# Norm, turning and router logits of a mixture-of-experts layer in one pipeline, and the router in one block

## The chip, the cores and the metric

The kernel runs on one core of a Trainium2 chip. The metric is the device time of one execution in microseconds (us), as the median of several runs. Engines: TensorE (PE, with its weight loads as PEld), VectorE (DVE), ScalarE (ACT), GpSimd (POOL), and SyncE (SP), which issues most of the DMAs.

## The reference, cut to what matters

Two transformer blocks over 1024 tokens of 1024 channels, float32. The change touches the head of the first block's mixture of experts (64 experts in 8 groups, top 2, hidden width 256):

```
h = rms_norm(x, norm_ffn)                       # 1024 x 1024
g_logits = h @ w_group + b_group                # 8 columns
g_sel, g_weight = argmax and its softmax share
e_logits = (h @ w_expert + b_expert)[group g_sel]   # 64 columns, 8 kept
top_w, top_local = top 2 of e_logits, softmax * g_weight
y = sum over both experts of weight * (silu(t @ w_gate) * (t @ w_up)) @ w_down
```

The assignments are sorted into blocks of 128 rows by expert; every expert's weights (3 MB) are read once.

## The kernel before, in words

The program is a sequence of blocks. In a block every engine runs its own list of instructions and waits on semaphores; at its end all engines meet. `c.recycle(0)` adds a block in which GpSimd clears and frees semaphores. `do = c.chain(...)` makes an engine wait for its own last instruction.

`moe_first` works through these stages for x, which lies in SBUF as 8 tiles (m) of 128 rows:

1. `load` fetches the norm's gain and waits for it. A further block issues the four loads of the router's weights `wr` (72 columns: 8 groups, 64 experts) and `bias` on SP.
2. `norm_transpose` (line 176): ScalarE squares and sums all 8 tiles, takes one root over all, and VectorE inverts it; then ScalarE scales tile m into one of 2 buffers `normed` and permutes its channels on the way (line 205: it writes single values 128 apart), SP stores the scaled tile to `ffn_rows` in DRAM (line 237), TensorE turns it in 8 pieces (line 228), VectorE multiplies it by the gain into `hT` (line 216). Reuse of a buffer waits for the turning and the store.
3. `route` (line 1787): SP issues the weights of the first two pairs of experts (12 DMAs of 1 MB), while TensorE makes the logits: for each m and k, hT is the stationary operand (128 columns), wr the moving one (72) (line 1813). The next blocks choose the group and both experts on VectorE, rank every assignment within its expert by matmuls with ones and a triangle (lines 1893, 1896), place them (lines 1907 to 1943), and turn the placement into lists `slot_tok`, `slot_row` with 16 one-hot matmuls (line 1950). There are seven blocks, so seven meetings. The third pair's weights are issued in the second.
4. The expert loop: `ExpertSteps` with 3 weight slots of a pair of experts and 32 steps. `clear_rows` zeroes the 3 row buffers in a block of its own (line 2346). GpSimd gathers 128 rows of `ffn_rows` per step and scatters results; TensorE turns the rows (line 2064) and makes the first product (line 2076) and the second (line 2097). SP refills a slot's gate and up weights when the slot's first product is done, its down weights when the second is done.
5. The overflow stage for experts with over 64 assignments, with its own buffers and `clear_rows`; then the sum into x.

The order of the work is written by hand throughout.

Of the kernel before, what the change touches and what calls it, by code (L numbers as in the profile page):

```python
# [17 lines left out]
P = 128  # L18
# [8 lines left out]
T = 1024  # L27
# [1759 lines left out]
def route(c, a, hT, w1, w2, slot_tok, slot_row, ov_expert, ov_count, weights,  # L1787
          wr, bias, loaded):
# [8 lines left out]
    NE = G + E  # L1797
    with ExitStack() as ctx:
        s = lambda n, shape, dt=F32: sbuf(ctx, nc, n, shape, dt)
        lg = s("rt_logits", [P, NT, NE])  # L1800
        ps = psum(ctx, nc, "rt_ps", 8)
        with nc.Block() as block:
            @block.sync
            def _(sp):
                for n in range(2):
                    load_expert_weights(sp, a, weights, n, 2, 2 * n)

            @block.tensor
# [23 lines left out]
        both, ones, before = s("rt_both", [P, NT, E], BF16), s("rt_ones", [P, P], BF16), s("rt_before", [P, P], BF16)  # L1832
        with nc.Block() as block:
# [5 lines left out]
            def _(pool):  # L1839
                it = lambda t, pat, base, mul: nc.gpsimd.iota(t, pat, base=base, channel_multiplier=mul,  # L1840
                                                              allow_small_or_imprecise_dtypes=True)
# [5 lines left out]
                nc.gpsimd.tensor_copy(ones[:], c.ones[:])  # L1847
                nc.gpsimd.tensor_copy(before[:], c.before[:])

            @block.vector  # L1850
            def _(dve):
                do = c.chain("vector", dve)
                do(nc.vector.tensor_tensor(lg[:], ps[:, :, :NE], bias[:].to_broadcast([P, NT, NE]), ALU.add))
                do(nc.vector.tensor_reduce(gm[:], lg[:, :, 0:G], AX, ALU.max))
                do(nc.vector.tensor_tensor(ex[:], lg[:, :, 0:G], gm[:].unsqueeze(2).to_broadcast([P, NT, G]),
                                           ALU.subtract))
        with nc.Block() as block:
            @block.scalar
            def _(act):
                nc.scalar.activation(ex[:], ex[:], ACT.Exp)  # L1860

            @block.vector
            def _(dve):
                do = c.chain("vector", dve)
# [1400 lines left out]
```

## Time and profile before

| | |
|---|---|
| median of 3 runs | 3776.32 us (3772.5 to 3778.88) |
| the profiled execution, its own time | 3779.07 us |
| its span in the profile | 3777.3 us |
| busy: PE, DVE, ACT, POOL | 85%, 37%, 24%, 4% of the span |
| granted TensorE clock, mean | 0.911 of full speed |
| stretch 1412.6 to 1540.6 us | from the end of the cross attention to the first expert product |

### The profile page before, as it was taken

The page shows a single profiled execution, that of the slowest core. Times are in us where ns is not written, and L with a number is a line of the kernel's source. Part 1 is how long each engine was busy: PE and PEld are TensorE (multiplying, and loading weights), DVE is VectorE, ACT ScalarE, POOL GpSimd, SP SyncE. Part 2 cuts the span into 40 slices and gives each one's busy share as a digit, 9 for nine tenths or more (in the row PEclk, how much of TensorE's full clock was granted, in tenths as well). Part 3 has the DMA queues.
Part 4 walks back from the last instruction along what each step waited for, and adds up shares of the span by engine and source line. Part 5 has one row for each costly group of instructions (what it writes and reads, how often), then busy time and mean ns, then how long its engine had stood idle before and what let it go on. Part 6 is the DMA issues. An engine that isn't in the chain of part 4 may idle for free. (4 is left out here: it accounts for less than half of the span.)

```text
span 3777.3 us, 36020 instructions
## 1 busy us (share of the span) xinstructions
PE 3201.8 (85%) x14454; PEld 2353.8 (62%) x14454; DVE 1405.4 (37%) x2144; ACT 925.2 (24%) x1477; POOL 156.7 (4%) x220
## 2 busy tenths in 40 slices
PE   7995777998766894787886489899999979999997
PEld 6784743445655774333332478778777768888886
DVE  3125835784241523210110663652223333333334
ACT  3324234443233402000000212003131132212211
POOL 0000011000000000111111030000000000000000
PEclk9997878999888995898998699999999989999999
DMA  3110000002210016599995403211111211111111
GB/s 92 45 42 9 1 12 1 1 1 84 87 61 28 1 34 248 224 420 421 417 414 228 164 26 77 65 50 45 39 45 45 78 50 51 45 50 50 45 51 73
DMA packets 138662, 370.27 MB, mean 98 GB/s; under 512 B 45120, under 2 KB 59328, under 8 KB 112384
## 3 DMA queue, kind: packets, MB, share of 16 engines
q1 hardware_dynamic: 129296, 351.38, 25.8%
q0 software_dynamic: 9216, 16.80, 1.2%
q8 instruction: 105, 1.72, 0.2%
q14 instruction: 45, 0.37, 0.0%
HBM read 352.92 MB, written 32.79 MB: 102 GB/s over the span
## 5 line engine op out<-in xcount | busy, mean ns | idle before, releaser
L2076 PE MATMUL moe_ph<-moe_wgu,moe_rowsT 128*64 128x512 f32 x1024 | 266.8, 681 | 65.5 <-DMA moe_wgu<-in_moe_w_up_dram 39.7
L509 PE MATMUL mlp_ps<-mlp_high,mlp_w_cut 128*128 128x512 f32 x1024 | 317.2, 391 | 6.0 <-DVE mlp_w_cut L424 6.0
L509 PE MATMUL mlp_ps<-mlp_w_cut,mlp_hidden_high 128*128 128x512 f32 x1024 | 315.2, 389 | 0.0
L424 DVE TENSOR_TENSOR m_w_cut<-m_w_raw,m_w_cut 128x512 fp32r<-128x512 f32 (+1 forms) x92 | 94.3, 1030 | 454.7 <-ACT m_w_cut L420 454.4
L2076 PEld LDWEIGHTS moe_ph<-moe_wgu,moe_rowsT 128*64 128x64 f32 x1024 | 91.2, 155 | 221.0 <-issue 194.7
L424 DVE TENSOR_TENSOR mlp_w_cut<-mlp_w_raw,mlp_w_cut 128x1024 fp32r<-128x1024 f32 x64 | 78.4, 1226 | 399.7 <-ACT mlp_w_cut L420 399.3
L420 ACT ACTIVATE m_w_cut<-m_w_raw 128x512 fp32r<-128x512 f32 (+1 forms) x92 | 76.3, 835 | 605.5 <-PE m_gates_ps L509 196.5
L509 PEld LDWEIGHTS mlp_ps<-mlp_high,mlp_w_cut 128*128 128x128 f32 x1024 | 193.4, 189 | 46.7 <-DVE mlp_w_cut L424 6.4
L509 PEld LDWEIGHTS mlp_ps<-mlp_w_cut,mlp_hidden_high 128*128 128x128 f32 x1024 | 192.2, 188 | 39.9
L509 PE MATMUL mlp_ps<-mlp_low,mlp_w_cut 128*128 128x512 f32 x512 | 200.1, 391 | 0.0
L509 PE MATMUL mlp_ps<-mlp_w_cut,mlp_hidden_low 128*128 128x512 f32 x512 | 199.2, 389 | 0.0
L420 ACT ACTIVATE mlp_w_cut<-mlp_w_raw 128x1024 fp32r<-128x1024 f32 x64 | 67.6, 1058 | 528.4 <-PE mlp_ps L509 525.9
L509 PE MATMUL m_cv_ps<-m_high,m_w_cut 128*128 128x512 f32 x512 | 165.4, 405 | 25.4 <-DVE m_w_cut L424 15.3
L2118 DVE COPY moe_hidT<-moe_pu 128x256 f32<-128x256 f32 x32 | 13.6, 425 | 443.4 <-PE moe_pu L2084 443.4
L509 PE MATMUL m_gates_ps<-m_high,m_w_cut 128*128 128x512 f32 x512 | 159.6, 393 | 4.1 <-DVE m_w_cut L424 4.1
L2097 PE MATMUL moe_py<-moe_wd,moe_hidT 128*64 128x512 f32 x512 | 116.9, 598 | 18.4 <-DVE moe_hidT L2118 17.6
L509 PEld LDWEIGHTS m_cv_ps<-m_high,m_w_cut 128*128 128x128 f32 x512 | 97.9, 194 | 49.6 <-DVE m_w_cut L424 16.8
L765 PE MATMUL mla_attn_scores<-mla_kT,mla_qT 96*128 96x512 f32 x256 | 120.4, 593 | 1.4 <-PEq L1374 1.4
L509 PE MATMUL mix_in_ps<-mix_high,mix_w_cut 128*128 128x512 f32 x384 | 121.2, 396 | 0.0
L509 PE MATMUL mix_in_ps<-mix_w_cut,mix_high 128*128 128x512 f32 (+1 forms) x384 | 113.6, 378 | 3.7 <-DVE mix_w_cut L424 3.7
L1708 DVE TENSOR_TENSOR x<-mlp_ps,x 128x512 f32<-128x512 f32 x128 | 87.0, 690 | 71.6 <-PE mlp_ps L509 71.6
L509 PEld LDWEIGHTS m_gates_ps<-m_high,m_w_cut 128*128 128x128 f32 x512 | 96.8, 189 | 26.7 <-DVE m_w_cut L424 4.5
(524 smaller groups left out, 6001.5 us busy)
## 6 DMA issues: line engine op xcount, KB each, us to landing
moe_wgu<-in_moe_w_gate_dram SPq DMA_DIRECT2D x64, 1024.0 KB, 20.2
moe_wgu<-in_moe_w_up_dram SPq DMA_DIRECT2D x64, 1024.0 KB, 24.7
moe_wd<-in_moe_w_down_dram SPq DMA_DIRECT2D x64, 1024.0 KB, 20.9
mlp_w_raw<-in_w_ff_dram SPq DMA_DIRECT2D x64, 512.0 KB, 3.5
m_w_raw<-in_w_in_dram SPq DMA_DIRECT2D x48, 256.0 KB, 2.8
mix_w_raw<-in_w_in_dram SPq DMA_DIRECT2D x40, 256.0 KB, 2.6
m_w_raw<-in_w_in_dram SPq DMA_DIRECT2D x20, 512.0 KB, 3.8
x_w_raw<-in_x_w_kv_dram SPq DMA_DIRECT2D x16, 512.0 KB, 3.7
```

The source lines that it names most:

```text
L420: nc.scalar.activation(part(s, 0).bitcast(F32R), raw(s), ACT.Copy).then_inc(high_ready, 1)
L424: nc.vector.tensor_tensor(part(s, 1).bitcast(F32R), raw(s), part(s, 0), ALU.subtract).then_inc(low_ready, 1)
L509: ins = nc.tensor.matmul(ps[:, b, :r.shape[-1]], l, r, start=(k == 0 and sw is high and wh == 0), stop=(k == job.nk - 1 and sw is low))
L765: ins = nc.tensor.matmul(ps_s[i % 2][:, s], qT[:, h, m * P:(m + 1) * P], kT[:, h, s * CH:(s + 1) * CH], start=True, stop=True)
L1708: return nc.vector.tensor_tensor(x[:, b, at], ps, x[:, b, at], ALU.add)
L2076: ins = self.nc.tensor.matmul(self.ps_h[r, i].rearrange("p (i n) -> p i n", i=2), self.rowsT[:, i, k, r], self.wgu[:, w * self.parts + h, ...
L2097: ins = self.nc.tensor.matmul(self.ps_y[r, half], self.hidT[:, i, k, r], self.wd[:, w * self.parts + h, k, half * CH:(half + 1) * CH], sta ...
L2118: self.nc.vector.tensor_copy(self.hidT[:, b % self.small].rearrange("p k t -> p (k t)"), self.ps_u[:, 0, :EH]).then_inc(self.hidT_ready, 1)
```

## The change

- The gain, router weights and biases are loaded by SP at the head of one block, the weights of the first two pairs of experts right behind them in the same queue.
- In that block, `router_logits`, the norm goes tile by tile: ScalarE sums and roots tile m + 3, VectorE inverts and scales (now with a `tensor_scalar` that writes single values 128 apart) into one of 3 buffers, ScalarE issues the store, TensorE turns, VectorE evacuates, TensorE makes the logits of the tile before. There wr is the stationary operand (72 columns) and hT the moving one (128), so the logits come out turned; ScalarE copies them in two halves, TensorE turns them back, VectorE adds the bias. TensorE waits for all five small loads first.
- `route` keeps its arithmetic but runs in one block: semaphores take the place of the meetings.
- The row buffers are zeroed inside the expert block, one by one, and a gather waits for its own. The overflow stage reuses the expert loop's buffers and doesn't zero them.

```diff
-def route(c, a, hT, w1, w2, slot_tok, slot_row, ov_expert, ov_count, weights,
-          wr, bias, loaded):
+def router_logits(c, a, x, hT, gain, weights, xn, wr, bias, lg):
...
+    c.recycle(0)
...
+    BUF = 3
...
+        ps, ps_l, ps_b = psum(ctx, nc, "ffn_ps", 4), psum(ctx, nc, "ffn_logitsT_ps", 2), psum(ctx, nc, "ffn_logits_ps", 2)
...
+        def take(act, h):
+            act.wait_ge(made, 4 * (h + 1))
+            nc.scalar.activation(lgT[:, h * CH:(h + 1) * CH], ps_l[:NE, h], ACT.Copy).then_inc(taken, 1)
...
             @block.sync
             def _(sp):
+                with nc.allow_non_contiguous_dma("small parameters"):
+                    for t, src in loads:
+                        sp.dma_start(t, src).then_inc(loaded, 16)
                 for n in range(2):
                     load_expert_weights(sp, a, weights, n, 2, 2 * n)
+                for b in range(BUF):
+                    sp.wait_ge(kept[b], 16 * len(range(b, NT, BUF)))
+
+            @block.scalar
+            def _(act):
+                def root(m):
+                    nc.scalar.activation(junk[:], x[:, m], ACT.Square, accum_out=ssq[:, m:m + 1]).then_inc(summed, 1)
+                    act.wait_ge(summed, m + 1)
+                    nc.scalar.activation(rstd[:, m:m + 1], ssq[:, m:m + 1], ACT.Sqrt, bias=c.eps[:, 0:1],
+                                         scale=1.0 / D).then_inc(rooted, 1)
+                for m in range(3):
+                    root(m)
+                for m in range(NT):
+                    act.wait_ge(row_ready, m + 1)
+                    nc.scalar.dma_start(xn[m * P:(m + 1) * P, :], normed[:, m % BUF]).then_inc(kept[m % BUF], 16)
+                    if m + 3 < NT:
+                        root(m + 3)
+                    if m % 4 == 0 and m:
+                        take(act, 0)
+                take(act, 1)
+            @block.vector
+            def _(dve):
+                def scale(m):
+                    dve.wait_ge(rooted, m + 1)
+                    nc.vector.reciprocal(rstd[:, m:m + 1], rstd[:, m:m + 1]).then_inc(inverted, 1)
+                    if m >= BUF:
+                        dve.wait_ge(turned, m - BUF + 1)
+                        dve.wait_ge(kept[m % BUF], 16 * (m // BUF))
+                    dve.wait_ge(inverted, m + 1)
+                    nc.vector.tensor_scalar(normed[:, m % BUF].rearrange("t (k p) -> t p k", p=P),
+                                            x[:, m].rearrange("t (p k) -> t p k", p=P), rstd[:, m:m + 1], None,
+                                            ALU.mult).then_inc(row_ready, 1)
+                scale(0)
+                scale(1)
+                dve.wait_ge(loaded, 16 * len(loads))
+                for m in range(NT):
+                    if m + 2 < NT:
+                        scale(m + 2)
+                    dve.wait_ge(turned, m + 1)
+                    nc.vector.tensor_tensor(hT[:, :, m * P:(m + 1) * P], sums(m),
+                                            gain[:].unsqueeze(2).to_broadcast([P, KD, P]),
+                                            ALU.mult).then_inc(evacuated, 1)
...
             @block.tensor
             def _(pe):
-                pe.wait_ge(*loaded)
-                for m in range(NT):
+                def logits(m):
+                    pe.wait_ge(evacuated, m + 1)
+                    at = slice(m * P, (m + 1) * P)
                     for k in range(KD):
-                        nc.tensor.matmul(ps[:, m, :NE], hT[:, k, m * P:(m + 1) * P], wr[:, k],
-                                         start=(k == 0), stop=(k == KD - 1))
+                        ins = nc.tensor.matmul(ps_l[:NE, m // 4, (m % 4) * P:(m % 4 + 1) * P], wr[:, k], hT[:, k, at],
+                                               start=(k == 0), stop=(k == KD - 1))
+                    ins.then_inc(made, 1)
...
+                pe.wait_ge(loaded, 16 * len(loads))
+                for m in range(NT + 1):
...
+                    if m:
+                        logits(m - 1)
+                    if m == 6:
+                        turn_back(0)
+                turn_back(1)
+
+def route(c, a, lg, w1, w2, slot_tok, slot_row, ov_expert, ov_count, weights):
...
+            @block.tensor
+            def _(pe):
+                pe.wait_ge(made, 7)
+                pe.wait_ge(picked, 1)
...
+                ins.then_inc(ranked, 1)
+                pe.wait_ge(placed, 1)
...
+                dve.wait_ge(made, 7)
                 pick_first(nc, do, lg[:, :, 0:G], gm[:], ids8[:], eq[:], gh[:])
...
-                do(nc.vector.tensor_tensor(both[:], flat[0], flat[1], ALU.add))
...
+                nc.vector.tensor_tensor(both[:], flat[0], flat[1], ALU.add).then_inc(picked, 1)
+                dve.wait_ge(exps_done, 2)
...
+                dve.wait_ge(ranked, 1)
...
+                ins.then_inc(placed, 1)
...
+                dve.wait_ge(filled, 1)
...
             st = ExpertSteps(c, run, "moe", a, xn, y, gain, slot_tok, slot_row, BUFS, 1, 2, 3, weights)
-            clear_rows(c, st.rows)
+            cleared = c.sem("moe_rows_cleared")
...
                     for n in range(3):
+                        pool.wait_ge(cleared, n + 1)
                         st.gather(pool, n, n, n)
...
+                    for b in range(BUFS):
+                        nc.vector.memset(st.rows[:, b], 0.0).then_inc(cleared, 1)
                     st.take_rowsT(dve, 0, 0)
...
-            st = ExpertSteps(c, run, "over", a, xn, y, gain, slot_tok, slot_row, 1, 1, 1, 1, one)
-            clear_rows(c, st.rows)
+            st = ExpertSteps(c, run, "over", a, xn, y, gain, slot_tok, slot_row, 1, 1, 1, 1, one, st)
```

In the pieces of the order of instructions below, - is the kernel before and + the changed one, each with its own line numbers.

TensorE, from the norm to the logits. `ffn_normed` holds the scaled tiles, `ffn_ps` the turned ones, `rt_w` the router's weights:

```order
-L228 MATMUL ffn_ps<-ident,ffn_normed 128x128 x64
-L190 UNCONDITIONAL_BRANCH
-L1808 UNCONDITIONAL_BRANCH
-L1813 MATMUL rt_ps<-rt_w,ffn_hT 128x72 x64
...
+L1899 MATMUL ffn_ps<-ident,ffn_normed 128x128 x16
+L1881 MATMUL ffn_logitsT_ps<-ffn_hT,rt_w 72x128 x8
+L1899 MATMUL ffn_ps<-ident,ffn_normed 128x128 x8
...
+L1881 MATMUL ffn_logitsT_ps<-ffn_hT,rt_w 72x128 x16
+L1888 MATMUL ffn_logits_ps<-ident,ffn_logitsT 128x72 x4
```

All turnings and then all logits are now turnings of tile m and logits of tile m - 1 in turn; the operands of the logits have changed places, and four turnings back follow each half.

VectorE, the same place; `ffn_hT` is the turned tile times the gain:

```order
-L212 RECIPROCAL ffn_rstd<-ffn_rstd 128x8
-L216 TENSOR_TENSOR ffn_hT<-ffn_ps,ffn_gain 128x8x128 x8
...
+L1851 RECIPROCAL ffn_rstd<-ffn_rstd 128x1
+L1856 TENSOR_SCALAR ffn_normed<-x,ffn_rstd 128x128x8
+L1867 TENSOR_TENSOR ffn_hT<-ffn_ps,ffn_gain 128x8x128
...
+L1872 TENSOR_TENSOR rt_logits<-ffn_logits_ps,rt_bias 128x288 x2
```

The scaling has come here; from the third tile on each tile is a reciprocal, a scaling and an evacuation of the tile two before.

ScalarE, the same place; `ffn_rows` is the copy in DRAM that the gathers read:

```order
-L195 ACTIVATE ffn_junk,ffn_ssq<-x 128x1024 x8
-L196 ACT_TABLE_LOAD
-L196 ACTIVATE ffn_rstd<-ffn_ssq,eps 128x8
-L197 ACTIVATE ffn_junk<-ffn_ssq 128x1
-L205 ACTIVATE ffn_normed<-x,ffn_rstd 128x128x8 x8
...
+L1833 ACTIVATE ffn_rstd<-ffn_ssq,eps 128x1
+L1840 DMA ffn_rows<-ffn_normed 128x1024
+L1831 ACTIVATE ffn_junk,ffn_ssq<-x 128x1024
...
+L1815 ACTIVATE ffn_logitsT<-ffn_logitsT_ps 72x512
```

One root for all tiles is now one per tile, the scaling is gone, and the stores, which were SP's, stand between the squares.

## Rows read from the trace of the kernel before

**Rows 1.** Windows: stretch, its us, busy us (count) by engine, granted clock, DMA share, GB/s
```profile
1432.00:1453.00 21.00, 14.08 (x64) 11.53 (x64) 9.80 (x8) 13.53 (x8) 0.00 (x0) 0.58 0.49 201
1453.00:1481.00 28.00, 27.55 (x128) 27.38 (x128) 0.07 (x1) 0.00 (x0) 0.10 (x1) 0.50 0.97 398
1481.00:1540.00 59.00, 11.54 (x84) 10.85 (x84) 35.10 (x101) 3.03 (x4) 5.17 (x14) 0.50 0.35 140
1540.00:1545.00 5.00, 4.39 (x12) 1.31 (x14) 0.56 (x1) 0.00 (x0) 1.21 (x2) 0.50 0.30 89
1545.00:1550.00 5.00, 5.00 (x24) 1.45 (x20) 0.00 (x0) 0.00 (x0) 0.00 (x0) 0.92 0.00 0
1600.00:2000.00 400.00, 327.10 (x1401) 126.29 (x1401) 46.68 (x74) 34.20 (x49) 59.09 (x96) 0.91 1.01 418
```

**Rows 2.** Timeline (start us, us, engine, line), end of cross attention to first root
```profile
1411.89 0.69 DVE L1708 TENSOR_TENSOR x<-x_out_ps,x 128x512 f32<-128x512 f32 x1 [0.67 <-PE x_out_ps L509]
...
1415.60 0.61 SPq L2188 DMA_DIRECT2D rt_w<-in_moe_w_group_dram  x1
...
1417.66 0.43 SPq L2188 DMA_DIRECT2D rt_bias<-in_moe_b_expert_dram  x1
1418.52 1.06 ACT L195 ACTIVATE ffn_junk<-x 128x1024 f32<-128x1024 f32 x1 [27.27 <-PEq L2184]
...
1427.94 1.28 ACT L196 ACT_TABLE_LOAD   x1
1429.24 0.30 ACT L196 ACTIVATE ffn_rstd<-ffn_ssq,eps 128x8 f32<-128x8 f32 x1
```

**Rows 3.** Groups of instructions, 1412 to 1541 us: count, busy us, mean ns, idle before
```profile
L205 ACT ACTIVATE ffn_normed<-x,ffn_rstd 128x1024 f32<-128x1024 f32 x8 | 15.5, 2031 | 4.5 <-DMA ffn_rows<-ffn_normed 4.3 <-DVE ffn_rstd L212 0.3
...
L216 DVE TENSOR_TENSOR ffn_hT<-ffn_ps,ffn_gain 128x1024 f32<-128x1024 f32 x8 | 9.8, 1225 | 12.9 <-PE ffn_ps L228 12.9
```

**Rows 4.** Timeline, router: VectorE and TensorE, idle before in brackets
```profile
1480.92 0.76 DVE L1853 TENSOR_TENSOR rt_logits<-rt_ps,rt_bias 128x576 f32<-128x576 f32 x1 [28.17 <-PEq L1802]
...
1484.01 0.23 DVE L1781 TENSOR_TENSOR rt_eq<-rt_logits,rt_gm 128x64 f32<-128x64 f32 x1 [1.81 <-PEq L1833]
...
1491.78 0.69 DVE L1882 TENSOR_TENSOR rt_both<-rt_picks 128x512 bf16<-128x512 f32 x1
...
1495.79 0.22 DVE L1907 TENSOR_REDUCE rt_gs<-rt_ex 128x8 f32<-128x64 f32 x1 [3.32 <-PEq L1883]
...
1496.89 0.22 DVE L1913 TENSOR_SCALAR rt_nb<-rt_ps 128x64 f32<-128x64 f32 x1
...
1513.10 2.22 DVE L1939 TENSOR_TENSOR rt_room<-rt_oend,rt_ids_over 128x1984 f32<-128x1984 f32 x1
...
1518.47 7.06 PE L1950 MATMUL rt_ps<-rt_picks,rt_atpos 128*128 128x63 f32 x32 [22.98 <-PEq L1901]
1525.83 0.22 DVE L1958 TENSOR_SCALAR rt_free<-rt_ps 128x63 f32<-128x63 f32 x1 [7.88 <-PEq L1944]
```

**Rows 5.** Timeline, clearing of the row buffers in both expert stages
```profile
1529.60 2.62 DVE L2346 MEMSET moe_rows<- 128x3072 f32 x1 [1.63 <-PEq L105]
...
1532.51 0.19 POOL L2038 COPY moe_itok<-slot_tok 128x1 int32<-128x1 int32 x1 [50.39 <-POOLq L2343]
...
2069.68 0.91 DVE L2346 MEMSET over_rows<- 128x1024 f32 x1 [15.60 <-PEq L105]
```

**Rows 6.** DMA issues 1400 to 1560 us (KB, us to landing), and landings of scatters
```profile
ffn_rows<-ffn_normed SPq DMA_DIRECT2D x8, 512.0 KB, 2.6
...
rt_bias<-in_moe_b_expert_dram SPq DMA_DIRECT2D x1, 32.0 KB, 3.9
...
DMA to landing us min/median/max: 2.7/8.3/18.8
```

**Rows 7.** Groups of instructions of VectorE, whole kernel, different shapes apart
```profile
L2591 DVE TENSOR_TENSOR m_u_cut<-m_last_side_ps,m_t_cut 128x512 fp32r<-128x512 f32 x8 | 8.9, 1158 | 0.0
...
L3054 DVE TENSOR_SCALAR m_t<-m_t,m_cw,m_cb 128x1024 f32<-128x1024 f32 x8 | 6.5, 811 | 0.1
```

More of the change, by code:

```diff
@@ new lines, in _ @@
+            @block.vector
[20 more added lines that the diff above has]
+                                            ALU.mult).then_inc(evacuated, 1)
+                for h in range(2):
+                    dve.wait_ge(back, h + 1)
+                    nc.vector.tensor_tensor(lg[:, 4 * h:4 * h + 4], ps_b[:, h, :4 * NE].rearrange(
+                        "p (m n) -> p m n", n=NE), bias[:].to_broadcast([P, 4, NE]), ALU.add)
@@ L1815, in route @@
+                turn_back(1)
+def route(c, a, lg, w1, w2, slot_tok, slot_row, ov_expert, ov_count, weights):
+    nc = c.nc
+    c.recycle()
+    with ExitStack() as ctx:
+        s = lambda n, shape, dt=F32: sbuf(ctx, nc, n, shape, dt)
         ids8, tok = s("rt_ids8", [P, NT, 8]), s("rt_tok", [P, NT])
@@ L1852, in _ @@
                 do = c.chain("vector", dve)
-                do(nc.vector.tensor_tensor(lg[:], ps[:, :, :NE], bias[:].to_broadcast([P, NT, NE]), ALU.add))
+                v = nc.vector
                 do(nc.vector.tensor_reduce(gm[:], lg[:, :, 0:G], AX, ALU.max))
[L1855 to L1864, printed above, removed]
+                nc.vector.tensor_tensor(ex[:], lg[:, :, 0:G], gm[:].unsqueeze(2).to_broadcast([P, NT, G]),
+                                        ALU.subtract).then_inc(exps, 1)
+                dve.wait_ge(made, 7)
                 pick_first(nc, do, lg[:, :, 0:G], gm[:], ids8[:], eq[:], gh[:])
@@ L1943, in _ @@
                 do(v.tensor_copy(ov_count, oend[0:1, 0, E - 1:E]))
-        with nc.Block() as block:
-            @block.tensor
-            def _(pe):
-                n = [(k, m) for k in range(2) for m in range(NT)]
-                for i, (k, m) in enumerate(n):
-                    nc.tensor.matmul(ps[:, 2, :NBLK], atpos[:, k, m], atblk[:, k, m], start=(i == 0),
-                                     stop=(i == len(n) - 1))
-        free, rowv, tokv = s("rt_free", [P, NBLK]), s("rt_rowv", [P, NBLK]), s("rt_tokv", [P, NBLK])
-        with nc.Block() as block:
-            @block.vector
-            def _(dve):
-                do = c.chain("vector", dve)
-                v = nc.vector
+                dve.wait_ge(filled, 1)
                 do(v.tensor_scalar(free[:], ps[:, 2, :NBLK], 0.0, 4.0 * T, ALU.is_equal, ALU.mult))
@@ L1996, with __init__ @@
 class ExpertSteps:
-    def __init__(self, c, ctx, name, a, xn, y, gain, slot_tok, slot_row, depth, small, parts, slots, weights=None):
+    def __init__(self, c, ctx, name, a, xn, y, gain, slot_tok, slot_row, depth, small, parts, slots, weights=None, like=None):
         self.nc, self.c, self.a, self.xn, self.y, self.gain = c.nc, c, a, xn, y, gain
@@ L2176, in moe_first @@
             bias = sbuf(tmp, nc, "rt_bias", [P, 1, NE])
[L2177 to L2191 removed]
+            lg = sbuf(tmp, nc, "rt_logits", [P, NT, NE])
+            router_logits(c, a, x, hT, gain, weights, xn, wr, bias, lg)
+            route(c, a, lg, w1[:], w2[:], slot_tok[:], slot_row[:], ov_expert[:], ov_count[:], weights)
         c.recycle(0)
@@ L2338, in _ @@
                                                            x[:, m - 1], ALU.mult, ALU.add).then_inc(added, 1)
-def clear_rows(c, rows):
-    nc = c.nc
-    with nc.Block() as block:
-        @block.vector
-        def _(dve):
-            nc.vector.memset(rows[:], 0.0)
 S5_RAW = 3 * PAIRS + 2 * PAIRS * SC
```

123 lines of the change are left out of this document (69 added, 54 removed).

## The prediction

> **What bounds the kernel now.** The windows of the profile come first, since the change touches one stretch of it, from the end of the cross attention at 1412.6 us to the first expert products at 1540.6 us. The reader should see there that no engine is busy all through that stretch and that it is a chain in series: ScalarE and TensorE take turns to 1453, then TensorE is alone for 28 us, then VectorE is busy for 35 of 59 us, and the DMA engines are full to 1481, at 0.35 in the mean to 1540, and empty from 1545 to 1550 [rows 1]. The window of the expert loop shows the opposite: 418 GB/s, DMA share 1.01 for 400 us [rows 1]. Its weights stream in through three slots that are filled beforehand; the fourth fill starts only when the first product is done. So the loop is a fixed length of transfer that begins when that product ends, and **a microsecond taken from the chain ahead of it moves the whole rest of the kernel by a microsecond**.
>
> **The clock origin.** The cross attention ends at 1411.89 + 0.69 = 1412.58 [rows 2]. A clearing of semaphores plus the start of a block takes 1.63 (the idle time ahead of the memset at 1529.60 [rows 5]). So the new block starts at T = 1414.2; now, one load block and its landing later, the first router weight is issued at 1415.60 and the first square starts at 1418.52 [rows 2]. Today the logits with bias stand in SBUF at 1480.92 + 0.76 = 1481.68 [rows 4], T + 67.5.
>
> **Term 1: norm, turning and logits as one pipeline.** What each engine does for a tile of 128 rows:
> - ScalarE: squares follow each other at (1427.94 - 1418.52)/8 = 1.18 us; the one table load is 1.28 and a root 0.30 [rows 2]. The first root is there at T + 2.8; after that 1.5 us a tile and a store issue of 0.3: never the limit.
> - VectorE takes the scaling from ScalarE. No row shows it writing single values 512 bytes apart. Bounds: 0.81 us, its tensor_scalar of 128x1024 with contiguous output [rows 7], and twice the 1.158 of a 128x512 operation whose input and output both step by 32 bytes, 2.3 us [rows 7]. ScalarE took 2.03 for this very pattern [rows 3], nearly 2 ns an element, and the 1.158 is about 2 ns an element too. I take 2.1. With a reciprocal of 0.2, the evacuation of 1.225 [rows 3] and gaps of 0.1, a tile is 3.6 us, eight are 29.
> - TensorE: the old product is two records per matmul, a load of 128 columns beside a stream of 72, 27.4/128 = 0.214 us each, at the granted clock 0.50, that is 1.2 GHz [rows 1]. The new one loads 72 and streams 128; the longer side is again 128, so I take 0.214 again: **making the weights stationary gains nothing by itself.** A tile is 8 turning records and 16 of logits, 24 x 0.214 = 5.1 us at 1.2 GHz, 2.6 at 2.4 GHz.
>
> So VectorE sets the pace at the high clock and TensorE at the low one. The chain at the high clock: the small loads need five issues and a landing, T + 0.4 + 2.06 + 3.9 = T + 6.4 [rows 2, 6]; row blocks 0, 1, 2 are scaled by T + 10.0. Block 3 needs a buffer back. The store of block 0 is issued near T + 6.4 and now runs beside 12 MB of expert weights, issued from T + 2.9 on. Alone such a store lands in 2.6 us [rows 6]; the loop's scatters, 512 KB to DRAM beside the weights, in 8.3 (2.7 to 18.8) [rows 6], which is the nearest row, so I take 8.3: block 3 is ready at T + 16.9, and then 3.6 us each, block 7 at T + 31.3. Two pieces of TensorE work and an evacuation later it is T + 37, its logits T + 39, and copy, four turns back, bias add (0.43, half of 0.76 and overhead) and block end give T + 41.4. With landings of 5 us the same sum gives T + 38.2. I take **T + 40: a gain of 27.5**. ScalarE's wait for half the logits stands ahead of the store of block 5, which nobody needs for a buffer: free.
>
> The Trainium skill (DMA: Bandwidth & Descriptors, Issuing engines are not separate DMA queues) speaks against the move of the stores to ScalarE: they run on the same 16 engines as the weights, and only issue time is saved. By it the stores do queue with the weights, as priced here; if moving them bought a free path, the sum would have the 2.6 us landing, T + 38.
>
> **Term 2: the router in one block.** Now VectorE idles 1.81 for a block change ahead of 1484.01 [rows 4]; instead it will wait for seven small GpSimd operations, done about 1.2 us after the block's start, when it is 0.5 into it itself: gain 1.0. It idles 3.32 for the ranking up to 1495.79 and then does the five operations for w1 and w2, 1.1 us, up to 1496.89; now these lie inside the wait: 1.1. A block change costs 0.3 (1518.47 + 7.06 to 1525.83); the two around the ranking go: 0.6. The 32 records of the last product, 7.06 us from 1518.47 at 1.2 GHz, start when the one-hot tiles are done at about 1513.3, beside the overflow arithmetic that runs from 1513.10 to 1518 (7.88 ahead of 1525.83) [rows 4]: gain 5.1, and 0.2 at the barrier behind it. Sum **8.0**. The third pair of weights is issued at this block's start; its 6 MB (15 us) stays hidden under 45 us.
>
> **Term 3: clearing inside the blocks.** The memset of 2.62 and the hop to GpSimd's first copy, 2.91 from 1529.60 to 1532.51 [rows 5], become one third of it and a hop, 1.0: gain **1.9**. The memset of the overflow stage, 0.91 [rows 5], and its block: gain **1.3**, with 0.4 for a block change, which took 0.3 in the router.
>
> **Sum:** 27.5 + 8.0 + 1.9 + 1.3 = 38.7. The profiled execution has a span of 3777.3; less 38.7 that is 3738.6. The median of the runs, 3776.32, is 1.0 below the span, so 3737.5. A difference under 0.2% (7.6 us) can't be told from none.
>
> **The rivals.**
> - *TensorE stays at 1.2 GHz.* For it: the 28 us of uninterrupted logit matmuls ran at 0.50 throughout, and so did the router [rows 1]. Against it: the new records stream 128 columns as the turning does, under which the clock rose in part (0.58 in the mean), and wide products lifted it to 0.92 within 5 us of their start [rows 1]. Then 5.1 us a tile from block 1 on give T + 53.5, a gain of 14 in term 1: 3751. The Trainium skill (TensorE: Matmul & The Clock Gate, Part 1) says that sustained matmul work releases the clock; by it the old 28 us should have run at 2.4 GHz, and the row says they did not. The trace decides, so this rival keeps a good chance.
> - *VectorE writes the stepped output at 0.81 and stores land soon.* 2.3 us a tile, T + 36: 3733.
> - *Stores land as the slowest scatter, 18.8.* The ring of three buffers makes three turns: the block ends at about T + 15 + 3 x landing = T + 71: 3769.
> - *Slower: the stores are served behind the weights.* Same place: ScalarE's store, VectorE's wait for a buffer, SP's wait at the block's end. Over T + 78.7 all gains are gone, which a landing of 21 us in each of three turns reaches. 12.6 MB at 418 GB/s are 30 us; with that landing T + 105: 3802. Against it: no scatter beside a full queue took over 18.8, and after the first turn the queue is drained.
> - *The change doesn't do what it says:* the loop absorbs the shift, as it would if its transfers had run on from before. Only term 3's end would be left, 3775. Against it: the DMA engines move nothing from 1545 to 1550, until the first product is done.
>
> **Chances:** forecast 0.58, low clock 0.24, fast VectorE 0.08, slow landings 0.04, behind the weights 0.03, no shift 0.03. Range: the low-clock case and 4 us for unseen block costs above, 3755; fast VectorE with somewhat more from the barriers below, 3727. The last three cases are left out of it. Faster 0.92, same 0.05 (no shift and half of the slow landings), slower 0.03.
>
> **What would show it.** The stepped tensor_scalar near 2.1 us x8; evacuations 3.6 us apart; logits in SBUF near T + 40 with the granted clock at 1.00 for most of the second half; last router product beginning before the overflow arithmetic ends; store landings of 5 to 9 us. Evacuations 5.1 us apart at clock 0.50 mean the low-clock rival; VectorE idle behind the stores means the landings. The prediction is wrong if the first expert product doesn't start between 1493 and 1520, or if the loop's rate is no longer 418 GB/s.

## The result and the profile after

The changed kernel takes **3745.36 us** (median of 4 runs, 3741.41 to 3748.14) against 3775.44 (3772.5 to 3778.88): ratio 0.992, interval 0.9905 to 0.9935, 30.1 us less. The forecast was 3737.5, 38.7 less. The profiled execution has its own time 3748.11 and a span of 3746.0 (before 3777.3), the granted clock is 0.917 in the mean.

Windows of the changed kernel (columns as in [rows 1]):

```profile
1425.00:1430.00 5.00, 5.00 (x27) 4.99 (x28) 2.76 (x4) 1.44 (x3) 0.00 (x0) 0.57 1.01 415
1430.00:1440.00 10.00, 6.34 (x44) 6.10 (x42) 4.85 (x6) 2.89 (x6) 0.00 (x0) 0.83 1.02 424
1440.00:1445.00 5.00, 4.67 (x43) 4.44 (x42) 3.51 (x4) 0.21 (x1) 0.00 (x0) 1.00 1.02 425
1445.00:1460.00 15.00, 10.53 (x94) 9.67 (x92) 7.06 (x9) 0.98 (x2) 0.00 (x0) 1.00 1.02 424
1480.00:1490.00 10.00, 0.00 (x0) 0.00 (x0) 9.65 (x41) 0.00 (x0) 0.00 (x0) 0.50 0.00 1
1600.00:2000.00 400.00, 321.39 (x1381) 121.16 (x1377) 43.38 (x69) 33.43 (x47) 57.77 (x94) 0.91 1.01 414
```

Norm and logits now overlap; the clock is at 2.4 GHz for most of the block's second half, where the logits stood at 1.2 GHz before. TensorE still stands idle for a quarter of the time from 1425 to 1460. Weights stream at 424 GB/s beside the pipeline, the third pair's are in soon after 1480 (DMA share 0.00), and the loop is nearly as it was: 414 GB/s in the same window, before 418. The timeline of the block:

```profile
1416.29 0.34 SPq L1822 DMA_DIRECT2D ffn_gain<-in_norm_ffn_dram  x1
...
1418.73 0.43 SPq L1822 DMA_DIRECT2D rt_bias<-in_moe_b_expert_dram  x1
1419.21 0.43 SPq L2085 DMA_DIRECT2D moe_wgu<-in_moe_w_gate_dram  x1
...
1424.97 3.68 PE L1899 MATMUL ffn_ps<-ident,ffn_normed 128*128 128x128 f32 x16 [10.31 <-DMA rt_bias<-in_moe_b_expert_dram]
...
1426.20 9.83 SPq L2089 DMA_DIRECT2D moe_wd<-in_moe_w_down_dram  x2
...
1432.91 1.33 DVE L1856 TENSOR_SCALAR ffn_normed<-x,ffn_rstd 128x1024 f32<-128x1024 f32 x1 [4.64 <-DMA ffn_rows<-ffn_normed]
...
1457.94 0.46 DVE L1872 TENSOR_TENSOR rt_logits<-ffn_logits_ps,rt_bias 128x288 f32<-128x288 f32 x1 [3.06 <-PE ffn_logits_ps L1888]
...
1461.88 0.22 DVE L1991 TENSOR_REDUCE rt_gm<-rt_logits 128x8 f32<-128x64 f32 x1 [3.49 <-PEq L1817]
```

And the scaled tile's instructions, stores and waits:

```profile
L1856 DVE TENSOR_SCALAR ffn_normed<-x,ffn_rstd x8: 1325/1362/1383, 1419.3 to 1447.7; 128x1024 f32<-128x1024 f32 x8
...
  DMA ffn_rows<-ffn_normed: 9.6, 5
...
DMA to landing us min/median/max: 9.2/11.8/13.7
```

Three things stand out. The last small load, with weights behind it in the queue, lands 6.2 us after its issue (before 3.9 [rows 6]), and TensorE waits for it. The stores land in 11.8 us instead of 2.6 [rows 6]; VectorE waits for them five times, 9.6 us: 4.6 for the first buffer that comes back, then 1.2 to 1.3 with every tile. And when the logits are done at 1458.40, the router does not start: the last store, issued at 1449.1, is still out, and the block's end waits 3.49 us for it.

The router and the first gather:

```profile
1490.41 2.22 DVE L2048 TENSOR_TENSOR rt_room<-rt_oend,rt_ids_over 128x1984 f32<-128x1984 f32 x1
1490.55 7.09 PE L1983 MATMUL rt_ps<-rt_picks,rt_atpos 128*128 128x63 f32 x32 [16.46 <-DVE rt_picks L2045]
...
1497.75 0.22 DVE L2054 TENSOR_SCALAR rt_free<-rt_ps 128x63 f32<-128x63 f32 x1 [2.49 <-PE rt_ps L1983]
```

The last product runs beside the overflow arithmetic, as forecast; VectorE idles 2.49 us for it instead of 7.88 [rows 4].

I compare kernels by stages, in us: *block*, from the issue of the gain's load (the "first issue" below) to the router's first reduction; *router*, from there to the end of the lists; *first product*, from the lists to the first expert product (1510.93 here). The stages come from one profiled execution each, the medians from all runs.

| kernel | block | router | first product | median |
|---|---|---|---|---|
| before (profiled twice) | 68.9, 66.7 | 46.3, 46.2 | 12.6, 12.7 | 3775.44, 3775.86 |
| the change (twice) | 45.6, 44.9 | 38.0, 38.0 | 11.0, 11.0 | 3745.36, 3743.03 |
| e1_weights_late | 32.5 | 38.0 | 13.6 | 3732.08 |
| e2_stores_not_at_end | 42.4 | 38.0 | 10.6 | 3738.01 |
| e3_stores_on_sp | 64.4 | 38.0 | 11.0 | 3763.59 |
| e4_rows_stationary | 42.8 | 38.0 | 11.1 | 3741.4 |
| e5_best_of_parts | 33.6 | 38.0 | 11.1 | 3730.14 |
| e6_router_block_only | 69.0 | 38.0 | 10.7 | 3763.97 |
| e7_stepped_read | 33.4 | 38.0 | 11.0 | 3729.48 |
| e8_small_loads_first | 40.4 | 38.0 | 11.0 | 3741.22 |
| e9_weights_placed | 30.8 | 38.0 | 11.0 | 3727.52 |
| e10_gain_alone | 30.6 | 38.0 | 10.7 | 3728.95 |

The loop, from the first product to its last scatter, took 517 to 520 us in all of them, the overflow stage 11.7 after and 13.0 before.

### The profile page after: what moved, and what is told of

Same layout as the page of the kernel before. It is cut to its first block and busy times, and to the rows that moved or that the text cites. A ratio compares the mean times of both kernels' runs of the same rounds, so it can differ in the third digit from the quotient of the medians.

```text
span 3746.0 us, 35945 instructions
## 1 busy us (share of the span) xinstructions
PE 3184.9 (85%) x14462; PEld 2336.8 (62%) x14462; DVE 1414.6 (38%) x2161; ACT 912.5 (24%) x1477; POOL 156.6 (4%) x220
## 5 line engine op out<-in xcount | busy, mean ns | idle before, releaser
L2177 PE MATMUL moe_ph<-moe_wgu,moe_rowsT 128*64 128x512 f32 x1024 | 261.9, 670 | 69.4 <-DMA moe_wgu<-in_moe_w_up_dram 42.8
L2219 DVE COPY moe_hidT<-moe_pu 128x256 f32<-128x256 f32 x32 | 13.6, 425 | 443.5 <-PE moe_pu L2185 443.5
## 6 DMA issues: line engine op xcount, KB each, us to landing
moe_wgu<-in_moe_w_up_dram SPq DMA_DIRECT2D x64, 1024.0 KB, 25.3
```

The costliest lines, as they stand in the source:

```text
L2177: ins = self.nc.tensor.matmul(self.ps_h[r, i].rearrange("p (i n) -> p i n", i=2), self.rowsT[:, i, k, r], self.wgu[:, w * self.parts + h, ...
L2219: self.nc.vector.tensor_copy(self.hidT[:, b % self.small].rearrange("p k t -> p (k t)"), self.ps_u[:, 0, :EH]).then_inc(self.hidT_ready, 1)
```

## The experiments

**1. The weights out of the block.** All three pairs are issued at the router's head.

```diff
-                for n in range(2):
-                    load_expert_weights(sp, a, weights, n, 2, 2 * n)
                 for b in range(BUF):
...
-                load_expert_weights(sp, a, weights, 2, 2, 4)
+                for n in range(3):
+                    load_expert_weights(sp, a, weights, n, 2, 2 * n)
```

> Edit: the changed kernel with the weights of the first two pairs of experts taken from the head of the norm block and issued at the head of the router block, ahead of the third pair. Theory A (the weights' transfer beside the pipeline is what the missing microseconds went to: last small load 2.2 us late, stores landing in 11.8 instead of 2.6 us, VectorE 9.6 us behind stores, and the block's end 3.5 us behind the last store): the last small load lands in about 4 us, the stores in 2.6 to 3.5 us, no wait of VectorE for a store, no idle time between the last bias add and the router; the stretch from the block's first issue to the router's first operation falls from 45.6 to 33 to 38 us, the first expert product moves with it, total 3735 to 3739. The 18 MB issued at the router's head need 43 us, but the first product needs only the first pair, 49 us later. Rival (the clock sets the pace: TensorE at 1.2 GHz needs 5.1 us a tile): the stretch stays over 43 us, total 3743 or more. Rival (the loop starves since its first weights come late): the first product waits for weights and the total is 3748 or more.

Measured 3732.08, ratio 0.9882 (0.9863 to 0.9901), less than the 3735 to 3739 of the theory. The block is 13.0 us shorter; the stores land in 3.3 us, near the 2.6 that they took before, and no wait of VectorE for a store is left:

```profile
L1838 ACTq DMA_DIRECT2D ffn_rows<-ffn_normed x8: 326/326/525, 1416.4 to 1433.1; - x8
...
DMA to landing us min/median/max: 2.6/3.3/5.8
```

What the weights cost in the block is shown with that. It also shows the pipeline's own pace: without store waits the evacuations follow each other every 2.6 to 2.9 us, in the change every 3.7 once the stores hold VectorE up. But 2.6 us come back before the first product. Windows of this run, from the first gather's issue on:

```profile
1485.80:1489.80 4.00, 0.00 (x0) 0.00 (x0) 0.91 (x1) 0.00 (x0) 2.65 (x4) 0.50 1.01 416
1489.80:1495.40 5.60, 1.97 (x8) 1.57 (x8) 1.23 (x1) 0.00 (x0) 1.47 (x3) 0.50 0.40 137
```

The queues were still full of weights at 1485.8, and TensorE got the gathered rows 6.27 us after the gather's issue (1492.12 from 1485.85) instead of 3.67 (1507.64 from 1503.97).

**2. The stores' wait out of the block's end.** `normed` lives on into the router, and VectorE waits for the stores ahead of its first reuse.

```diff
-                for b in range(BUF):
-                    sp.wait_ge(kept[b], 16 * len(range(b, NT, BUF)))
...
                 nc.vector.tensor_tensor(m2[:], m2[:], m1[:], ALU.subtract).then_inc(exps, 1)
+                for b in range(3):
+                    dve.wait_ge(stores[1][b], 16 * len(range(b, NT, 3)))
```

> Edit: the changed kernel with the wait for the stores of the scaled rows taken off the end of the norm block; the buffers live on and the router waits for the stores before it reuses their place, 7 us into its block. Theory: the 3.5 us that all engines idle between the last bias add (1458.4) and the router's first operation (1461.9) are the landing of the last store: they go down to about 0.5, everything behind moves by 3 us, total 3742. Rival (the idle time is the start of the block and its code, not the store): nothing moves, total 3745.

Measured 3738.01, ratio 0.9897 (0.9878 to 0.9916). The block is 3.2 us shorter, and the router starts 0.30 after the last bias add instead of 3.49, so that is the price of the last store's landing. (The median lies 7.4 us below the change's first one and 5.0 below its second; what it gains beyond the 3.2 is not explained.)

```profile
1454.93 0.46 DVE L1870 TENSOR_TENSOR rt_logits<-ffn_logits_ps,rt_bias 128x288 f32<-128x288 f32 x1 [3.06 <-PE ffn_logits_ps L1886]
...
1455.69 0.22 DVE L1989 TENSOR_REDUCE rt_gm<-rt_logits 128x8 f32<-128x64 f32 x1 [0.30 <-PEq L1817]
```

**3. The stores on SP, behind the weights.**

```diff
-                    act.wait_ge(row_ready, m + 1)
-                    nc.scalar.dma_start(xn[m * P:(m + 1) * P, :], normed[:, m % BUF]).then_inc(kept[m % BUF], 16)
...
                     load_expert_weights(sp, a, weights, n, 2, 2 * n)
+                for m in range(NT):
+                    sp.wait_ge(row_ready, m + 1)
+                    sp.dma_start(xn[m * P:(m + 1) * P, :], normed[:, m % BUF]).then_inc(kept[m % BUF], 16)
```

> Edit: the changed kernel with the stores of the scaled rows issued by SP behind the weights instead of by ScalarE. Theory of separate rings: in one ring the stores wait for all 12.6 MB ahead of them, so the first lands about 33 us after the block's start, VectorE waits for it with the fourth tile, and the stretch from the block's first issue to the router grows from 45.6 to 52 to 60 us, total 3752 to 3760. Rival (the issuing engine doesn't matter, the transfers share the same 16 engines either way): stores land in 9 to 14 us as now, total 3745 within 3.

Measured 3763.59, ratio 0.9966 (0.9954 to 0.9979): 18.8 us more in the block, more than either theory said. SP stood in its weight issues until 1428.5, though tile 0 had been scaled 12 us before; the first three stores landed 22.9 to 24.8 us after their issue, just behind the last of the weights (in at 1452.1), and VectorE waited 29.4 us at one place. SP's rows (the second puts all eight stores together):

```profile
1421.92 6.59 SPq L2090 DMA_DIRECT2D moe_wd<-in_moe_w_down_dram  x2
1428.56 37.52 SPq L1827 DMA_DIRECT2D ffn_rows<-ffn_normed  x8
```

The same stores, VectorE's wait for them and their landing:

```profile
L1827 SPq DMA_DIRECT2D ffn_rows<-ffn_normed x8: 319/320/2136, 1428.6 to 1465.8; - x8
...
  DMA ffn_rows<-ffn_normed: 29.4, 1
...
DMA to landing us min/median/max: 2.6/3.4/24.8
```

This is the mechanism of the rival that ended slower, for one turn of the ring. On ScalarE's queue no store took over 13.7 us beside the same weights. The Trainium skill (DMA: Bandwidth & Descriptors, Issuing engines are not separate DMA queues) says that all issuers share 16 engines and that another issuer saves only issue time, usually little. The sharing is there (11.8 against 2.6 us), but here the other issuer saves 18.8 us, and the measurement decides.

**4. The rows stationary again.** No copies, no turns back.

```diff
-                        ins = nc.tensor.matmul(ps_l[:NE, m // 4, (m % 4) * P:(m % 4 + 1) * P], wr[:, k], hT[:, k, at],
+                        ins = nc.tensor.matmul(ps_b[:, m // 4, (m % 4) * NE:(m % 4 + 1) * NE], hT[:, k, at], wr[:, k],
...
-                    dve.wait_ge(back, h + 1)
+                    dve.wait_ge(made, 4 * (h + 1))
```

> Edit: the changed kernel with the operands of the logits back in their old places (the turned rows stationary, 128 columns loaded; the router's weights moving, 72 columns), so that the logits come out unturned: no copy by ScalarE, no turning back. Theory 1 (the operands' places matter only through the clock): with 72 columns streamed beside each load the granted clock stays at 0.50 longer, TensorE needs up to 5.1 us a tile and becomes the limit, the stretch from first issue to router 48 to 56 us, total 3748 to 3756. Theory 2 (the stores set the pace and the end, the places are worth nothing): the stretch is 45.6 less the copies and turns that stood behind the last tile, 0 to 2 us shorter, total 3743 to 3746, whatever the clock.

Measured 3741.4, ratio 0.9907 (0.9889 to 0.9926), the block 2.8 us shorter. The missing copies and turns are not what made it shorter. In both runs the block's end waits for the last store; that went out 32.7 us after the first issue here and 32.8 in the change, and landed in 9.6 us here and 12.3 there. The logits were ready 41.2 us after the first issue instead of 42.1, and the block waited for the store:

```profile
1455.80 0.46 DVE L1869 TENSOR_TENSOR rt_logits<-ffn_logits_ps,rt_bias 128x288 f32<-128x288 f32 x1 [1.94 <-PE ffn_logits_ps L1878]
...
1457.87 0.22 DVE L1985 TENSOR_REDUCE rt_gm<-rt_logits 128x8 f32<-128x64 f32 x1 [1.62 <-PEq L1817]
```

Why that store landed sooner is not shown; the same store of the unchanged change took 12.0 in its second profile. At 2.4 GHz the 16 records take 1.90 us either way. But after TensorE's wait of 3.6 us for tile 1 the clock stood at 1.2 GHz for 10.2 us in this run, in the change for 3.4 after the same wait:

```profile
1434.75:1444.98 10.23, 10.23 (x52) 10.23 (x50) 7.23 (x9) 1.47 (x4) 0.00 (x0) 0.50 1.02 424
```

Experiment 9 returns to this.

**5. The parts together.** Experiment 4's edit, and the weights between both places: the first pair once the last tile is scaled, two pairs at the router's head.

```diff
+                sp.wait_ge(row_ready, NT)
+                load_expert_weights(sp, a, weights, 0, 2, 0)
                 for b in range(BUF):
...
+                for n in (1, 2):
+                    load_expert_weights(sp, a, weights, n, 2, 2 * n)
```

> Rows of hT stationary again (as in the fourth run), and the weights placed between the two places tried so far: the first pair's issued in the norm's block once the last row tile is scaled, the other two pairs' at the router's head. Theory (the parts add, and the 2.6 us that the first experiment gave back before the first expert product were its first gather's landing beside weights still in flight, 5.9 against 3.3 us): the norm's block takes 30.5 to 31.5 us (32.6 less the copies and turns at its end), the weights are all in about 5 us before the lists are, the first gather lands in 3.3 to 4 us, the first expert product comes 11.0 to 11.7 us after the lists, and the time is 3727 to 3730. Rival: the first pair's weights delay the last three stores, the block's end waits for these or for SyncE that stands in its issues, and the block takes 34 us or more: 3731 to 3735.

Measured 3730.14, ratio 0.9881 (0.9863 to 0.9898). The queues are at a quarter when the gathers start (DMA share 0.25 from 1480 to 1485), and the first product comes 11.1 us after the lists: the cause of the 2.6 us is shown. But the block takes 33.6 us, between the theory's 31 and the rival's 34. The last small load took 4.6 us instead of 3.8, and the clock rose late, though that cost little: from the first turning to the router it is 26.5 us here and 26.2 in experiment 1. Windows of this run from the first turning on:

```profile
1416.10:1419.60 3.50, 3.49 (x17) 3.48 (x18) 2.89 (x5) 2.92 (x7) 0.00 (x0) 0.50 0.82 323
1419.60:1425.30 5.70, 5.70 (x29) 5.70 (x29) 4.18 (x5) 2.84 (x6) 0.00 (x0) 0.50 0.46 182
1425.30:1442.50 17.20, 16.48 (x150) 16.33 (x149) 11.68 (x14) 0.05 (x1) 0.00 (x0) 1.00 0.64 247
```

**6. The router's block and the clearing alone.** Norm, logits and the weights' issue as before, each in its block.

```diff
-            router_logits(c, a, x, hT, gain, weights, xn, wr, bias, lg)
+    load(c, [(gain[:], a["norm_ffn"][0].rearrange("(p k) -> p k", p=P))])
...
+    norm_transpose(c, "ffn", x, hT, gain, NT, keep=xn)
...
+                        ins = nc.tensor.matmul(ps[:, m, :NE], hT[:, k, m * P:(m + 1) * P], wr[:, k],
```

> The kernel before with only the router's one block and the moved clearing: norm, turning, stores and logits stand as before, the weights go out at the logits as before. Theory (the terms add): the router takes 38.0 us from its first operation instead of 46.3, the first expert product comes about 11 us after the lists instead of 12.6, the overflow stage 1.3 us less: 10 to 12 us below the kernel before of the same job, 3765 to 3767. Rival: part of the change's 30 us was shared between the parts (the router's shorter stretch brings the first gather beside weights in flight, as in the first experiment), so that this part alone gives 7 to 9: 3768 to 3770.

Measured 3763.97, ratio 0.9976 (0.9963 to 0.9988), 10.8 us under the kernel before of the same job (3774.8), as the first theory has it (10 to 12): the terms add, as far as the medians can tell.

**7. A stepped read for the stepped write,** on experiment 5.

```diff
-nc.vector.tensor_scalar(normed[:, m % BUF].rearrange("t (k p) -> t p k", p=P),
-                        x[:, m].rearrange("t (p k) -> t p k", p=P), rstd[:, m:m + 1], None,
+nc.vector.tensor_scalar(normed[:, m % BUF].rearrange("t (k p) -> t k p", p=P),
+                        x[:, m].rearrange("t (p k) -> t k p", p=P), rstd[:, m:m + 1], None,
```

> As the run e5_best_of_parts, but the scaling on VectorE writes its output in order and reads its input in steps of 8 elements, instead of reading in order and writing in steps (same values at the same places). Theory (a step costs the same on either side): the operation stays at 1.3 to 1.4 us, the time within 1 us of e5. Rival (only a stepped write costs): about 0.8 us an operation; the time still within 2 us of e5, since TensorE's 2.6 us a row tile is the next bound.

Measured 3729.48, ratio 0.9876 (0.9858 to 0.9893), not to be told from experiment 5. The operation falls between both theories (1.3 to 1.4 and 0.8):

```profile
L1853 DVE TENSOR_SCALAR ffn_normed<-x,ffn_rstd x8: 1145/1168/1185, 1412.8 to 1432.5; 128x1024 f32<-128x1024 f32 x8
```

**8. The small loads first,** with the change's early weights.

```diff
+                sp.wait_ge(loaded, 16 * len(loads))
                 for n in range(2):
                     load_expert_weights(sp, a, weights, n, 2, 2 * n)
```

> The change with one edit: SyncE waits until the five small loads have landed before it issues the experts' weights; the place of the weights, at the norm's head, is kept otherwise. Theory (4 to 5 us of the block are the small loads' landing behind the first weights, 8.7 us after the block's first issue instead of 3.9 to 6.3, and the stores' landing is the rest): TensorE starts 2.5 us earlier or more, the waits of VectorE for stores stay, the block takes 42 to 44 us instead of 45.6, and the time is 3742 to 3744. Rival (the stores' landing beside the weights sets the pace whatever the start): the block stays at 45 to 46 us, 3745.

Measured 3741.22, ratio 0.9912 (0.9897 to 0.9926). The block is 4.5 to 5.2 us shorter, more than expected; the waits for stores (8.3 us) and at the end stay:

```profile
1414.92 1.33 PE L1900 MATMUL ffn_ps<-ident,ffn_normed 128*128 128x128 f32 x5 [7.03 <-DMA rt_bias<-in_moe_b_expert_dram]
...
1449.96 0.22 DVE L1992 TENSOR_REDUCE rt_gm<-rt_logits 128x8 f32<-128x64 f32 x1 [2.89 <-PEq L1817]
```

TensorE begins 5.4 us after the first issue instead of 8.7 and 8.4, so 3.0 to 3.3 of the gain are the earlier start; of the rest, 1.1 to 1.3 are shorter waits for stores.

**9. Experiment 5 with the router's weights stationary.** This is the change with one edit, experiment 5's place for the weights.

> The change with one edit, the place of the experts' weights as in e5_best_of_parts (first pair once the last row tile is scaled, the other two at the router's head); the router's weights are stationary, as in the change. It differs from e5 only in the operands of the logits. Theory (which operand is stationary decides how soon the granted clock rises: in the runs so far it rose 4.5 to 5.5 us after TensorE's first operation with the router's weights stationary and nothing to wait for, 9.2 with the rows stationary in e5 and e7): it rises within 6 us of the first transpose, the norm's block takes 32 to 33 us instead of e5's 33.6, although it has the copies and turns, and the time is 3728 to 3730. Rival (the placement or chance made the difference): the clock rises after 9 us, the block takes 34.5 to 35.5, the time is 3731 to 3733.

Measured **3727.52**, ratio 0.9884 (0.9867 to 0.9901); the change itself took 3743.03 in the same job. Windows from the first turning on:

```profile
1413.90:1417.40 3.50, 3.46 (x16) 3.45 (x17) 3.06 (x6) 3.15 (x8) 0.00 (x0) 0.50 0.75 295
1417.40:1423.10 5.70, 5.70 (x51) 5.70 (x51) 5.43 (x7) 4.01 (x9) 0.00 (x0) 0.96 0.65 258
1423.10:1439.20 16.10, 14.64 (x136) 14.26 (x134) 10.09 (x12) 1.31 (x4) 0.00 (x0) 1.00 0.71 249
```

This pair of runs does not settle what the operands are worth. The clock rose here 3.9 us after the first turning, 0.5 after the first logits had begun, so nearly all that TensorE had done until then was the same turnings as in experiment 5. Likewise it rose 0.7 us after the first logits in experiment 4, with the rows stationary. Other runs tell more, since in them the first logits ran on at 0.50. In experiment 1, with the router's weights stationary, the clock rose 2.5 us into the logits:

```profile
1420.97:1423.42 2.45, 2.45 (x13) 2.45 (x13) 2.44 (x3) 1.16 (x4) 0.00 (x0) 0.50 0.46 184
1423.42:1426.80 3.38, 3.38 (x33) 3.38 (x32) 3.05 (x4) 2.17 (x6) 0.00 (x0) 1.00 0.61 246
```

In experiments 5 (its windows above) and 7, with the rows stationary, it rose only 5.9 and 5.8 us into them, TensorE busy throughout. With experiment 4's 10.2 us against 3.4 and the 28 us of old logits in which it never rose [rows 1], the runs speak for it that the clock comes back sooner with the router's weights stationary, though they are few. What that is worth is little: the block is 2.8 us shorter than in experiment 5, of which 1.6 are the small loads' earlier landing (first turning 5.5 after the first issue, there 7.1), and 1.2 are left. Experiments 9 and 1, with the same operands, differ by nearly as much behind their first turnings (25.3 and 26.2 us). The difference of the times, 2.6 us, lies within what two jobs differ by.

**10. The gain's own semaphore,** with the stepped read, on experiment 9.

```diff
-                dve.wait_ge(loaded, 16 * len(loads))
+                dve.wait_ge(gained, 16)
...
-                pe.wait_ge(loaded, 16 * len(loads))
                 for m in range(NT + 1):
+                    if m == 1:
+                        pe.wait_ge(loaded, 16 * (len(loads) - 1))
```

> As e9_weights_placed, with the stepped read of e7 and a semaphore of its own for the gain vector: the transposes wait for the scaled row alone, VectorE's evacuations for the gain (the first load issued), only the logits for the router's weights. Theory (the start of the pipeline is set by the last small load): the first transpose comes 2 to 3 us sooner after the block's first issue (4.5 instead of 7.1), the block takes 30 to 31 us, the time 3726 to 3728. Rival: the first logits wait for the router's weights instead, TensorE stands idle between its first transposes and these, the clock rises later for it, and the block takes 32 to 34 us: 3729 to 3731.

Measured 3728.95, ratio 0.9882 (0.9866 to 0.9899). The first turning starts 4.2 us after the first issue instead of 5.5, but the block takes 30.6, only 0.2 less than in experiment 9, and the time shows nothing. The first logits then run at 1.2 GHz for their first 1.5 us (2.69 us for 16 records, there 2.15):

```profile
1416.04 2.69 PE L1883 MATMUL ffn_logitsT_ps<-ffn_hT,rt_w 128*72 128x128 f32 x16 [0.28 <-DVE ffn_hT L1868]
```

**11. The change once more,** beside experiments 9 and 10.

> The change as it is, beside the two runs above on the same chip. If the runs compare from call to call: 3744 to 3747, ratio to before 0.991 to 0.993, the norm's block 45 to 46 us. It also shows once more how far the place of the block's start in the span moves from run to run with nothing changed ahead of it (1408 to 1415 us so far).

Measured 3743.03 (3734.18 to 3746.29), ratio 0.9918 (0.9903 to 0.9933), block 44.9.

**12. The kernel before once more.**

> The kernel before, profiled a second time. In the profiled executions the change's kernel reached the end of the cross attention 2.8 us later than the kernel before (1415.4 against 1412.6), with no changed instruction ahead of that point; its own later profiles and those of its variants reach it at 1407.0 to 1414.2. Theory (this is the scatter of single executions): the kernel before reaches it somewhere from 1407 to 1415 too, and takes 660 to 661 us from there to the end of the expert stages, as in its first profile. Rival (the change delays what is ahead of it, or the stretch itself scatters by 4 us): it reaches the point at 1412 to 1413 again, or the stretch differs from 660.5 by over 2 us.

Measured 3775.86 (3773.17 to 3780.48), ratio 1.001 (1.0 to 1.0019). It ends the cross attention at 1411.5, but the stretch from there to the end of the overflow stage is 657.5 us, 3.0 shorter than in its first profile. 2.2 of that lie in the block, 1.4 of them in the logits: here the clock was at 2.4 GHz when they began, and fell in them for good.

```profile
1449.31:1452.72 3.41, 1.83 (x16) 1.59 (x16) 1.23 (x1) 0.00 (x0) 0.00 (x0) 1.00 0.40 101
1452.72:1477.30 24.58, 24.58 (x116) 24.38 (x115) 0.00 (x0) 0.00 (x0) 0.00 (x0) 0.50 1.00 417
```

The first half of the theory held, the second did not: the stretch itself scatters by 3 us.

## Why the prediction was right and where it was wrong

**Right:** the direction, the range, the place, and that a microsecond saved ahead of the loop moves all that follows. The first product came at 1510.93, between the 1493 and 1520 that were named. Term 2 was 8.0 and is 8.3; VectorE's wait for GpSimd's constants, 0.76, took the place of an idle 1.81 as priced. Term 3 was 1.9 and 1.3 and is 1.6 and 1.3. Experiment 6 has both terms without the first: 10.8 us in the time.

**Wrong by a size: term 1.** 27.5 was forecast; the profiles show 22.6 (68.9 less 45.6, less 0.6 for a later start), 21.1 in the second pair. By the forecast's own steps, with T at 1417.0 (the end of the cross attention, 1415.39, and 1.63):
- *The small loads at T + 6.4* came at T + 7.9, landing in 6.2 us instead of 3.9 since weights stand behind them. The price of the unloaded row was taken for a loaded queue. Experiment 8 starts TensorE 3.0 to 3.3 us earlier by this alone.
- *Block 3 at T + 16.9, block 7 at T + 31.3* came at T + 17.2 and T + 32.1. That is luck, since the errors behind it cancel: the first store left at T + 4.5 instead of T + 6.4, it landed in 11.3 us instead of 8.3, and the stepped write took 1.36 us instead of 2.1. Also *"VectorE sets the pace at the high clock"* was wrong. VectorE's own work for a tile was forecast at 3.6 us, and 3.7 were measured, but 1.2 to 1.3 of these are its wait for a store; where no store holds it up (experiments 1 and 9), evacuations are 2.6 us apart for most of the block, the 2.6 that the forecast gives TensorE at 2.4 GHz.
- *Logits and block end at T + 41.4, taken as T + 40:* the logits were there at T + 41.4, the block ended at T + 44.9. **This step failed:** the landing was priced where a buffer comes back and not where the block ends. The last store leaves at T + 32.1, and with the median landing of 11.8 us the block can't end before T + 43.9. Experiment 2 takes 3.2 us there.
- *"Making the weights stationary gains nothing by itself"* held for a record's duration (16 take 1.90 or 1.91 us at 2.4 GHz) and, as far as the runs can show, for the time. That the clock seems to come back sooner with it (experiment 9) was not forecast.

**The rivals.** TensorE at 1.2 GHz fell: 1.00 from 1440 to 1460. The rival with the fast stepped write was half right: 1.36 us is nearer its 0.81 than 2.1, but its stores were to land soon and took 11.8. As slow as the slowest scatter, 18.8, no store was. Stores behind the weights did not come about, but experiment 3 makes them: 3763.59. The loop did not absorb the shift: 518.8 us, 519.5 before.

**The rest.** The stages add up to a gain of 34.4 us in the first pair of profiles and 32.3 in the second; the medians show 30.1 and 29.9. Point and length of unchanged stretches move by some us from one execution to the next (the cross attention ended between 1407.0 and 1415.4 in the profiled ones), so 2 to 4 us of this account stay open.

## What to carry to other kernels

A bulk prefetch that starts early is not free when the code beside it has small loads and stores on its critical path: ask for each landing that somebody waits for, the block's end among them, what it costs beside a full queue. Issue the bulk once the last such transfer is out, and early enough that it has drained before the next one: this placement alone took the change from 3743.03 to 3727.52 us. Stores that give back buffers belong on an issuer that has no bulk in front of them.

## What the runs showed of the hardware

- Behind bulk in the same queue a transfer waits for it, and its issuer stands: SP stood 9.83 us in two issues of 1 MB with ten ahead of them (the change), and three stores behind the weights landed 22.9 to 24.8 us after their issue, 1.3 to 3.7 after the last weight (experiment 3). On another queue the same stores took 8.6 to 13.7 us beside the weights (four profiles), and 2.6 to 5.8 with nothing beside them (experiment 1).
- Standing ahead of bulk in the queue does not protect a small load: the last one, 32 KB, landed in 5.9 to 6.3 us with weights issued right behind it (five profiles) and in 2.9 to 4.6 with none behind it (nine profiles).
- Scaling 128x1024 float32 on VectorE takes 1.36 us with a write in steps of 512 bytes, 1.17 with a read in steps of 32 bytes, 0.81 in order [rows 7]; ScalarE takes 2.03 for the same write [rows 3].
- With TensorE busy without a gap from the first turning on, the granted clock rose after 3.9 and 5.9 us with 72 columns loaded and 128 streamed in the logits (experiments 9 and 1), and after 9.4 and 9.3 us with the operands exchanged (5 and 7). The operands are not all: with them exchanged it also rose once after 4.2 us (experiment 4). Logits alone with the rows stationary ran 28 us at 0.50, and in the second profile of before lost a clock of 1.00 after 1.5 us and stood at 0.50 for the other 24.6. At 1.2 GHz a logit record takes 0.21 us either way.
